# Idle TensorE products in the waits for x, and x's remainders ahead of a weight's, in a four-layer encoder kernel

## The reference

```python
for layer in range(DEPTH):
    p = x @ w_in[layer]
    mixed = mixer(p)
    recalled = _memory_attention(q, mem, mem_w_kv[layer])
    y = jnp.concatenate([mixed, recalled], axis=-1) @ w_o[layer]
    x = _layer_norm(ALPHA * x + y, ln_gain[layer, 0], ln_bias[layer, 0])
    f = _conv_ffn(x, ffn_w_up[layer], ffn_conv[layer], ffn_w_down[layer])
    x = _layer_norm(ALPHA * x + f, ln_gain[layer, 1], ln_bias[layer, 1])
```

## Time and profile before

| | us |
|---|---|
| median of 3 runs | 1337.62 |
| lowest, highest | 1337.5, 1342.72 |
| the profiled execution | 1340.19 |
| its span, first to last instruction | 1338.3 |
| mean granted clock of TensorE in it | 0.989 |

### The profile page before, as it was taken

One profiled execution on the slowest core, in us unless ns is written; L12 is line 12 of the kernel. 1 busy time (PEld: TensorE's weight loads), 2 busy tenths in 40 slices (PEclk: granted clock), 3 DMA queues, 4 the chain that ended last, 5 costly groups with the idle time before them and its releaser, 6 DMA issues.

```text
span 1338.3 us, 20850 instructions
## 1 busy us (share of the span) xinstructions
PE 1299.3 (97%) x7958; PEld 1143.2 (85%) x7958; DVE 1026.0 (77%) x1604; ACT 709.1 (53%) x1102; POOL 67.0 (5%) x92
## 2 busy tenths in 40 slices
PE   7999999999989999999999999999999999899998
PEld 6998888888989998888888898888888997788886
DVE  4675888888678767888888677888888665788887
ACT  4763665555742233655554644655554763555553
POOL 0001000000024430000000000000000000000000
PEclk8999999999989999999999999999999999899999
DMA  7643475554442233565554564765554533475551
GB/s 280 234 140 114 154 232 181 187 188 160 158 142 96 80 112 125 179 237 186 186 188 142 173 242 138 237 206 189 184 181 154 192 130 96 141 240 187 185 189 63
DMA packets 63391, 228.31 MB, mean 171 GB/s; under 512 B 7446, under 2 KB 9110, under 8 KB 62268
## 3 DMA queue, kind: packets, MB, share of 16 engines
q1 hardware_dynamic: 63292, 226.97, 51.2%
HBM read 225.88 MB, written 1.06 MB: 170 GB/s over the span
## 4 chain that ended last, share of the span: by engine, by line
PE 87%; DVE 7%; ACT 2%; issue 2%; DMA 1%; POOL 0%; SPq 0%; DVEq 0%; ACTq 0%; POOLq 0%
PE pair L600 25%; PE pair L602 12%; PE acc L641 8%; PE acc L643 7%; PE acc L642 7%; PE pair L613 5%; PE pair L614 5%; PE pair L615 5%; PE pair L813 3%; DVE w_lo L1026 2%; PE pair L625 2%; PE pair L629 2%; PE pair L627 2%; DVE y_tok L1191 1%; PE acc L714 1%
## 5 line engine op out<-in xcount | busy, mean ns | idle before, releaser
L1026 DVE TENSOR_TENSOR w_lo<-raw,w_hi 128x1024 fp32r<-128x1024 f32 x404 | 488.0, 1221 | 146.5 <-ACT w_hi L830 143.1
L830 ACT ACTIVATE w_hi<-raw 128x1024 fp32r<-128x1024 f32 x404 | 424.1, 1057 | 246.6 <-PE acc L643 121.7
L600 PE MATMUL pair<-xT,w_hi 128*128 128x512 f32 x1408 | 498.5, 398 | 0.9 <-DVE xT L1171 0.7
L602 PE MATMUL pair<-xT,w_lo 128*128 128x256 f32 x1408 | 395.3, 281 | 0.0
L600 PEld LDWEIGHTS pair<-xT,w_hi 128*128 128x128 f32 x1408 | 265.0, 188 | 66.4 <-issue 1.8
L602 PEld LDWEIGHTS pair<-xT,w_lo 128*128 128x128 f32 x1408 | 266.5, 189 | 1.3
L613 PE MATMUL pair<-xT,w_hi 128*128 128x256 f32 x592 | 173.7, 293 | 2.4 <-DVE xT L1171 2.4
L614 PE MATMUL pair<-xT,w_hi 128*128 128x256 f32 x592 | 170.0, 287 | 0.0
L615 PE MATMUL pair<-xT,w_lo 128*128 128x256 f32 x592 | 169.7, 287 | 0.0
L642 PE MATMUL acc<-w_lo,gT_hi 128*128 128x512 f32 x352 | 139.1, 395 | 0.0
L641 PE MATMUL acc<-w_hi,gT_hi 128*128 128x512 f32 x352 | 138.9, 395 | 0.0
(11 more groups left out here) (163 smaller groups left out, 1624.2 us busy)
## 6 DMA issues: line engine op xcount, KB each, us to landing
raw<-in_stream SPq DMA_DIRECT2D x404, 512.0 KB, 4.1
gains<-in_ln SPq DMA_DIRECT2D x8, 1024.0 KB, 8.5
bias<-bias_scratch SPq DMA_DIRECT2D x2, 1152.0 KB, 7.8
x_tok<-in_x SPq DMA_DIRECT2D x2, 512.0 KB, 4.9
y_tok<-in_mem SPq DMA_DIRECT2D x1, 1024.0 KB, 11.2
out<-x_tok SPq DMA_DIRECT2D x4, 256.0 KB, 2.0
masks_in<-in_masks_c SPq DMA_DIRECT2D x1, 512.0 KB, 7.5
fconv_w<-in_fconv SPq DMA_DIRECT2D x1, 264.0 KB, 7.5
```

What stands on the lines that cost most here:

```text
L600: pe.matmul(bank, w_hi[:, slot, at], xT[:, k].rearrange("p a s -> p (a s)"), start=(k == 0), stop=(k == KT - 1), skip_group_check=True)
L602: last = pe.matmul(bank[:, 0:SEQ], w_lo[:, slot, at], xT[:, k, 0, :], start=False, stop=(k == KT - 1), skip_group_check=True)
L830: nc.scalar.activation(w_hi[:, u % SPLIT, :], raw[:, u % RAW, :], ACT.Copy).then_inc(hi_ready, 1)
L1026: v.tensor_tensor(w_lo[:, u % SPLIT, :], raw[:, u % RAW, :], w_hi[:, u % SPLIT, :].bitcast(F32), ALU.subtract).then_inc(lo_ready, 1)
```

## The change

Three edits.

- At the start PE does two further products of zeros after the turn of x's first tile and three after that of the second (`WARM_X`). Each is a float32 product of 512 columns into ACC[0], which nobody reads and which the first user clears.
- In norm 6 alone, a new item `("warm",)` between the turn of the first half and that of the second: PE multiplies 16 times mixT_hi by itself (512 columns, fp32r) into the half bank PROJ that the next chunk will clear. Ahead of it PE waits until the bank's last user has been read.
- In `close`, `("lo", 2 * c + AHEAD)` moves on DVE's list: where a chunk follows, from ahead of the first half's turn to behind it; where none does, behind the turns of both halves.

```diff
@@ make_schedule, close @@
-            items.extend([("stats", m, 1), ("norm", m, 1), ("lo", 2 * c + AHEAD)])
+            items.extend([("stats", m, 1), ("norm", m, 1)])
             if not last:
                 items.append(("turn", m, 0))
             if following:
+                items.append(("lo", 2 * c + AHEAD))
                 chunks.append(following)
                 items.extend([("half", c + 1, 0), ("part", c + 1)])
+            elif not last:
+                items.append(("warm",))
             items.append(("hi", 2 * c + 1 + AHEAD))
             if not last:
                 items.append(("turn", m, 1))
             if following:
                 items.append(("half", c + 1, 1))
+            else:
+                items.append(("lo", 2 * c + AHEAD))
             items.append(("lo", 2 * c + 1 + AHEAD))
@@ tensor block @@
+            def idle_work(count):
+
+                for _ in range(count):
+                    pe.matmul(ACC[0][:], zeros[:, 0:P], zeros[:], start=True, stop=True)
+
             pe.wait_ge(consts_ready, 3)
-            for _ in range(WARM_UP):
-                pe.matmul(ACC[0][:], zeros[:, 0:P], zeros[:], start=True, stop=True)
+            idle_work(WARM_UP)
...
+                elif name == "warm":
+
+                    n = proj_ord[last_half + 1]
+                    pe.wait_ge(*proj_read(n - 2))
+                    for _ in range(WARM_NORM):
+                        pe.matmul(PROJ[n % 2], mixT_hi[:, 0, 0:P], mixT_hi[:, 0:2, :].rearrange("p a s -> p (a s)"),
+                                  start=True, stop=True)
...
                         last.then_inc(turned, 1)
+                    if what == "x":
+                        idle_work(WARM_X[t])
```

More of the change, by code:

```diff
@@ L47 @@
 WARM_UP = 2
+WARM_X = (2, 3)
+WARM_NORM = 16
 RAW, SPLIT, AHEAD = 5, 5, 4
@@ L670, in _ @@
                 if name == "half":
+                    last_half = item[1]
                     half(item[1], item[2], pos)
+                elif name == "warm":
[4 more added lines that the diff above has]
+                                  start=True, stop=True)
                 elif name == "part":
```

## The result

| us | before | changed |
|---|---|---|
| median | 1337.88 (6 runs, 1337.5 to 1342.72) | 1326.78 (6 runs, 1325.45 to 1328.53) |
| profiled execution, its span | 1340.19, 1338.3 | 1326.18, 1324.4 |
| mean granted clock in it | 0.989 | 0.999 |

The ratio is 0.9907, with a 95% interval of 0.9891 to 0.9923: faster by 0.8 to 1.1%. The forecast was 1327.8 and the range 1324.2 to 1332.5.

A forecast was written before the change was run, and what follows sets the result against it. TensorE (PE) bounds the kernel, losing time where it waits or runs at the lower clock. Gains of 1.35 + 2.6 + 2.9 + 3.0 = 9.85 us take the median from 1337.62 to 1327.8, range 1324.2 to 1332.5.

The forecast's parts named there:

- The start: Products of zeros keep the full clock; chunk 0 ends 2.25 us earlier, of which the wait for bias_rows leaves 1.35.
- rival (b): Behind the start, PE's new 1.6 us hole after L695 lets the clock fall anew: 1329.5 to 1331.3 us, chance 0.12.
- Norms 0 to 5: Moving the weight's remainder gives 0.85 us in each of norms 0, 2, 4 and 0.97 in each of 1, 3, 5.
- Norm 6: Norm of layer 3's output projection: order and sixteen products give 3.0 us with the clock held, 1.1 without.
- Rival (e): Norm 6 alone loses the clock, transposes not holding it, and gives 1.1 in place of 3.0: 1329.7 us, chance 0.10.
- (d): The low-clock stretch in layer 1's level stage goes away, 3.5 us more won: 1324.3 us, chance 0.07.
- (c): More low-clock stretches in layer 1's level stage, each up to 3.5 us; 1341.8 us with four, chance 0.03.
- (a): Clock not held: products of zeros take 1.69 us each, start loses 0.35, norm 6 gives 1.1; 1331.4 us, chance 0.13.

The follow-up runs named there:

- order_only: Against the kernel before, only the move of the weight's remainder on DVE's list, no added products: 1331.03 us, ratio 0.9953.
- warm_only: Against the kernel before, only the sixteen products in norm 6: 1335.65 us, ratio 0.9989.
- warm_transposes: The changed kernel with 34 transposes in place of the sixteen products in norm 6: 1328.79 us, ratio 0.9929 to the kernel before.
- start_only: Against the kernel before, only the five products of zeros at the start: 1338.76 us, ratio 1.0015.
- bias_first: The changed kernel with weight unit 5 rounded after bias_rows and the turn of mem: 1326.06 us, ratio 0.9904 to the kernel before.
- x_overrun: The changed kernel with six products of zeros after x's second tile in place of three: one execution, 1329.8 us.
- lo_behind_both: The changed kernel with the weight's remainder behind x's remainders of both halves in all seven norms: 1335.37 us, ratio 0.9982 to the kernel before.
- after_again: The changed kernel measured again with no edit, beside the kernel before: 1328.18 us, ratio 0.9922.

## Why the prediction was right, point by point

**The start: 1.35 forecast, 1.09 and 1.28 measured where the clock held, and -0.25 to -0.77 where it did not.** The steps are as written: products at 0.85 once the clock is up, the second transposes in 1.04, chunk 0 ended 1.98 us earlier (2.25), the copy of bias_rows stands behind the rounding of unit 5 (20.92 for 20.65), and PE idles 1.65 us (1.6). Two things were sized wrong. The first L613 did not stay at 12.71. In all kernels with three products or none it came 4.0 to 4.4 us behind the start of x's second turn, and that start moved from 7.99 to 9.06 (8.33 before). In the changed kernel's profile it stands right behind the two products, which ended at 8.78 and not at 7.5, because the clock was still low when they began; so they may have delayed it. And rival (b) had a chance of 0.12; it happened in four of eight profiles. It cost 1.1 to 2.1 us against those that held, which is what its 3.4 us at the lower clock come to. With the falls the start gives 0.29 on average and the old start 0.38, so that 1.35 was met in the profiles in which the clock held is luck: the term as a gain of the change was wrong by all of it. The forecast of the total stood because 1.35 is small beside the rest.

**Norms 0 to 5: 5.5 forecast, 6.06 measured (3 x 0.88 and 3 x 1.14).** In 0, 2 and 4 the step is exact: the second pair of xT behind w_lo is what the next chunk waits for, and it comes 0.88 earlier (0.85). In 1, 3 and 5 I took 0.97 between the bounds 0.81 and 1.14, and it is the upper one. What was misread is the idle time: 0.81 in the earlier trace rows counts from the modelled end of the product before, but the next can start before that end. PE turned 0.97 earlier, and its transposes took 0.17 less on top.

**Norm 6: 3.0 forecast, 2.55 and 2.96 measured.** L607 came 1.60 earlier (1.6), made of 1.13 from the order (order_only) and 0.46 from the products (warm_only), which is the split that the prediction gave. The rest, 1.4 forecast, is 0.95 or 1.36, a difference of one of the 0.4 us steps. Rival (e) was wrong, and warm_transposes shows why: transposes held the clock. The profile of before had a short fall there, 6.8 us; start_only, with the same code, lost 1.26 us more in one of 10.2. So against another execution of the kernel before the norm would have given over 4.

**Layer 1: 0 forecast, 4.28 in the pair of profiles.** This is (d), with a chance of 0.07 and 3.5 us. I take it for luck and not for the change's: no edit touches the stage, the same kernel measured again fell there once, and bias_first, with all edits, fell there just as the kernel before did. The profile of the kernel before was one with two falls (2.6 and 1.6 us), and that of the changed kernel one with none; the wait of 1.18 us is in both. So the two spans differ by 13.93 us while the medians differ by 11.1. The right sum to hold against the forecast of 9.85 is the stages that the change touches: 1.09 + 2.64 + 3.42 + 2.55 = 9.7 us. Of these 6.06 repeat in every profile, and the rest hangs on where the clock fell in the one profile of before. That the medians moved by 11.1 and 11.2 us and not by 9.85 is within the range; no run says what the last microsecond is.

**The rival that ended slower, (c), did not happen**, nor did (a): no products of zeros ran at half speed after a turn, except for the beginning of the first in three profiles (2.15 us for the two in the changed kernel's, 1.97 in x_overrun's, 2.33 in lo_behind_both's, for 1.88), where the transposes before them took 1.91 us.

What stays open: the steps of 0.4 us, what sets whether POOL or DVE is served first in layer 1, and what sets whether the clock falls behind a given hole of 1.6 us in a given execution.

## What to carry to other kernels

An engine's place in an ordered list is cheap to change and its gain repeats to two hundredths of a microsecond (0.88 and 1.14, ten profiles); but move an item no further than its own reader allows, for one turn further lost 6.5 us. Filling a wait with unread work pays only if the time won is not spent as a new, emptier wait behind it: look at what the next engine in the chain is queued behind, and move that too (bias_first). Where a clock falls by luck, don't compare two spans; compare the starts of the same instructions, stage by stage, and put aside the stages that no edit touches.

## What the runs showed of the hardware

- Float32 transposes held the full clock as well as products did (3.9 us of them in a row and 8 more on either side, clock 1.00), where 5.29, 4.15 and 2.78 us of idle let it fall. Idle time of 1.6 to 1.8 us did not let it fall in warm_only's norm 6, and did in half of the profiles behind L695. At the old start it fell at 9.6 in warm_only and at 9.8 in order_only, where PE had idled 1.67 and 1.98 us and then transposed for 1.06.
- The granted clock of a window says 1.00 before its first record too. At the very start it was the lower level: two products of zeros took 3.4 to 3.8 us there and 1.88 once the clock was up, and in the changed kernel's profile the first eight transposes took 1.91 us and not 1.04. When it first rises differs from execution to execution of the same work.
- Each fall of the clock ahead of the kernel's last microseconds was 3.4, 6.8 or 10.2 us long, and where PE had work it cost up to half of that. In layer 1 one of 3.4 us cost 1.1 to 1.6 us and one of 6.8 us 2.6. Its price can be hidden: in after_again the wait of 1.18 us for POOL behind it was not there, so that the layer came out as in the profile without a fall.
- POOL and DVE slowed each other on like work at the same time (128x256 float32): POOL's first instruction took 0.73 us with DVE's beside it at 0.91, or 1.64 with DVE's at 0.41. In 6 of the 14 profiles POOL was the late one at one level of layer 1, and PE waited 1.17 or 1.18 us for it.
